# Sums of squares of the head norms in a two-block transformer kernel: one float32 matmul replaced by two fp32r matmuls of a split square

## The reference, cut to what matters

```
def _rms(x, g):
    xf = x.astype(jnp.float32)
    y = xf * lax.rsqrt(jnp.mean(xf * xf, axis=-1, keepdims=True) + EPS)
    return (y * g.astype(jnp.float32)).astype(x.dtype)

k = _rms(k, k_norm_g)                                      # 16 heads of 128, FoX keys
q = _rms(q.reshape(bsz, s, B_HEADS, HEAD_DIM), q_norm_g)   # 16 heads of 128, FoX queries
q = rms_norm(q.reshape(b, t, A_HEADS_2, HEAD_DIM_2), q_g)  # 8 heads of 64, second block
k = rms_norm(k.reshape(b, t, A_KV_HEADS, HEAD_DIM_2), k_g) # 2 heads of 64, second block
```

## Time and profile before

| | value |
|---|---|
| median of three runs | 1354.71 us (1353.22 to 1357.62) |
| profiled execution | 1361.22 us, its span 1359.5 us |
| TensorE matmul busy | 1253.9 us, 92% |
| DVE busy | 794.2 us, 58% |
| ACT busy | 613.7 us, 45% |
| POOL busy | 107.8 us, 8% |
| granted TensorE clock, mean | 0.958 of full |
| DMA | 219.93 MB, mean 162 GB/s |

### The profile page before, as it was taken

The page is one execution under the profiler, slowest core; times in us unless marked ns, Lnnn a source line. Parts: engine busy times, 40 slices in busy tenths (PEclk is TensorE's granted clock), DMA queues, the critical chain, the costliest instruction groups (busy, mean ns, idle before and its releaser), DMA issues.

```text
span 1359.5 us, 20850 instructions
## 1 busy us (share of the span) xinstructions
PE 1253.9 (92%) x8513; PEld 1146.1 (84%) x8513; DVE 794.2 (58%) x1257; ACT 613.7 (45%) x950; POOL 107.8 (8%) x172
## 2 busy tenths in 40 slices
PE   1799999898979899999989598999999999899998
PEld 1799999876878899887788378999989987899997
DVE  6786998654486354455446746555555433665554
ACT  2447623433455454554434335444444554544442
POOL 0100000022030000011100410000000133000000
PEclk9999999997979999999979688999999999899999
DMA  9796789501647556322532044555554321455552
GB/s 321 223 310 200 230 261 312 200 1 34 198 150 226 153 162 204 104 92 94 163 94 70 32 155 131 181 187 187 187 183 149 131 94 62 155 186 186 187 186 93
DMA packets 164879, 219.93 MB, mean 162 GB/s; under 512 B 5868, under 2 KB 135696, under 8 KB 164784
## 3 DMA queue, kind: packets, MB, share of 16 engines
q1 hardware_dynamic: 163984, 216.82, 49.3%
q0 software_dynamic: 800, 1.77, 0.4%
HBM read 217.53 MB, written 1.05 MB: 161 GB/s over the span
## 4 chain that ended last, share of the span: by engine, by line
PE 75%; DVE 11%; DMA 6%; ACT 5%; issue 2%; SPq 0%; DVEq 0%; ACTq 0%
PE ps L636 12%; PE ps L640 11%; PE ps L637 11%; PE ps L693 6%; PE ps L694 6%; PE ps L698 6%; DMA raw_weights<-in_a_w_in 3%; PE ps L666 3%; PE ps L667 3%; DVE w_lo L1543 3%; PE ps L671 3%; DVE acc L1626 2%; ACT w_hi L1223 1%; PE ps L924 1%; DMA raw_weights<-in_kv_w 1%
## 5 line engine op out<-in xcount | busy, mean ns | idle before, releaser
L1543 DVE TENSOR_TENSOR w_lo<-raw_weights,w_hi 128x1024 fp32r<-128x1024 f32 x348 | 423.9, 1229 | 291.4 <-ACT w_hi L1223 289.9
L1223 ACT ACTIVATE w_hi<-raw_weights 128x1024 fp32r<-128x1024 f32 x348 | 362.6, 1054 | 415.3 <-PE ps L698 110.3
L636 PE MATMUL ps<-act_hi,w_hi 128*128 128x256 f32 x1664 | 418.5, 289 | 6.4 <-ACT w_hi L1223 6.4
L637 PE MATMUL ps<-act_lo,w_hi 128*128 128x256 f32 x1664 | 410.1, 284 | 0.0
L636 PEld LDWEIGHTS ps<-act_hi,w_hi 128*128 128x128 f32 x1664 | 320.5, 193 | 14.1 <-issue 10.4
L637 PEld LDWEIGHTS ps<-act_lo,w_hi 128*128 128x128 f32 x1664 | 320.7, 193 | 3.5 <-issue 2.9
L640 PE MATMUL ps<-act_hi,w_lo 128*128 128x256 f32 x1664 | 234.7, 284 | 5.8 <-DVE w_lo L1543 5.8
L640 PEld LDWEIGHTS ps<-act_hi,w_lo 128*128 128x128 f32 x1664 | 215.5, 193 | 6.4 <-DVE w_lo L1543 6.4
L693 PE MATMUL ps<-w_hi,act_hi 128*128 128x512 f32 x360 | 142.7, 396 | 2.3 <-DVE work L1728 1.7
L694 PE MATMUL ps<-w_hi,act_lo 128*128 128x512 f32 x360 | 141.2, 392 | 0.0
L698 PE MATMUL ps<-w_lo,act_hi 128*128 128x512 f32 x360 | 99.2, 389 | 0.0
(11 more groups left out here) (252 smaller groups left out, 1295.6 us busy)
## 6 DMA issues: line engine op xcount, KB each, us to landing
raw_weights<-in_ffn_w SPq DMA_DIRECT2D x66, 1024.0 KB, 5.3
raw_weights<-in_a_w_in SPq DMA_DIRECT2D x32, 1024.0 KB, 6.1
raw_weights<-in_mod_w SPq DMA_DIRECT2D x24, 1024.0 KB, 5.8
raw_weights<-in_kv_w SPq DMA_DIRECT2D x16, 1024.0 KB, 5.8
raw_weights<-in_b_w_in SPq DMA_DIRECT2D x16, 1024.0 KB, 5.4
raw_weights<-in_od_w_qkv SPq DMA_DIRECT2D x12, 1024.0 KB, 5.1
raw_weights<-in_kv_mod_w SPq DMA_DIRECT2D x8, 1024.0 KB, 5.5
raw_weights<-in_a_w_out SPq DMA_DIRECT2D x8, 1024.0 KB, 4.9
```

The source lines that it names most:

```text
L636: pe.matmul(dst, wh[:, k, :], act_hi[:, base + k, :], start=(k == 0), stop=False)
L637: pe.matmul(dst, wh[:, k, :], act_lo[:, base + k, :], start=False, stop=False)
L1223: act.activation(half_view(w_hi, s), HALVES[s][2], ACT.Copy).then_inc(hi_done, 1)
L1543: dve.tensor_tensor(half_view(w_lo, s), HALVES[s][2], half_view(w_hi, s).bitcast(F32), ALU.subtract).then_inc(lo_done, 1)
```

## The change

TensorE gets two fp32r matmuls for each sum: the square rounded to fp32r, and the exact rest of it. POOL makes both, with a cast and a subtraction of 128x512. The rounded part has one buffer, the rest two, in the memory of `h_sq` and of the second `h_r` buffer, so `h_r` has one buffer left and ACT waits for the previous unit's read of it. The constant matrices become a tile of fp32r type, which is read as float32 where float32 is wanted; their first part is loaded on POOL's queue at the start of its program in place of SP's, the second part by two transfers in place of one.

```diff
+        cst_r = sb("cst_matrices", [P, 5 * P], F32R)
+        cst = sb("cst_rows", [P, const.shape[1] - 5 * P])
+        with nc.sbuf_tensor("work_rounded", [P, 3584], F32R) as work_r:
+            pass
...
-        h_r = work[:, 1024:2048].rearrange("p (b n) -> p b n", b=2)
+        h_r = work[:, 1024:1536]
+        h_sq_hi = work_r[:, 1536:2048]
+        h_sq_lo = work_r[:, 0:1024].rearrange("p (b n) -> p b n", b=2)
...
         @block.gpsimd
+            pool.dma_start(cst_r[:, 0:256], const[:, 0:256].bitcast(F32R)).then_inc(ident_in, 16)
...
-            pool.dma_start(cst[:, 256:], const[:, 256:]).then_inc(masks_in, 16)
+            pool.dma_start(cst_r[:, 256:], const[:, 256:640].bitcast(F32R)).then_inc(masks_in, 16)
+            pool.dma_start(cst[:, :], const[:, 640:]).then_inc(masks_in, 16)
...
-            for h in range(HA):
-                if h == KD:
-                    pool.wait_ge(unit_ready, FIRST["q"] + 8)
-                split_output(h, o_full[:, h % 2, :], st("fx_out"), st("fx_split"), fox_chunk(h))
+            def split_squares(n):
+                pool.wait_ge(st("hsq_ready"), n + 1)
+                if n >= 1:
+                    pool.wait_ge(st("hssq_ready"), n)
+                pool.tensor_copy(h_sq_hi, h_sq[:, n % 2, :]).then_inc(st("hsq_hi"), 1)
+                pool.wait_ge(st("hsq_hi"), n + 1)
+                pool.tensor_tensor(h_sq_lo[:, n % 2, :], h_sq[:, n % 2, :], h_sq_hi.bitcast(F32), ALU.subtract)\
+                    .then_inc(st("hsq_lo"), 1)
+            for n in range(8):
+                split_squares(n)
+            for i in range(2, HA + 6):
+                if i % 2 == 0 and i <= HA:
+                    split_squares(8 + (i - 2) // 2)
+                if i >= 6:
+                    h = i - 6
+                    if h == KD:
+                        pool.wait_ge(unit_ready, FIRST["q"] + 8)
+                    split_output(h, o_full[:, h % 2, :], st("fx_out"), st("fx_split"), fox_chunk(h))
+            for n in range(16, 19):
+                split_squares(n)
...
             def head_square_sums(mat, count):
-                pe.wait_ge(st("hsq_ready"), count + 1)
+                pe.wait_ge(st("hsq_lo"), count + 1)
...
-                pe.matmul(square_bank(count), mat, h_sq[:, count % 2, :], start=True, stop=True)\
+                pe.matmul(square_bank(count), mat, h_sq_hi, start=True, stop=False)
+                pe.matmul(square_bank(count), mat, h_sq_lo[:, count % 2, :], start=False, stop=True)\
                     .then_inc(st("hssq_ready"), 1)
...
         @block.sync
-            sp.dma_start(cst[:, 0:256], const[:, 0:256]).then_inc(ident_in, 16)
...
             def scale_unit(n, size):
-                if n >= 2:
-                    wait_read(act, *normed_units[n - 2])
+                if n >= 1:
+                    wait_read(act, *normed_units[n - 1])
...
-            dve.wait_ge(masks_in, 32)
+            dve.wait_ge(masks_in, 48)
```

More of the change, by code:

```diff
@@ L154, in build @@
         acc = sb("acc", [P, 2, HALF])
-        cst = sb("cst", [P, const.shape[1]])
+        cst_r = sb("cst_matrices", [P, 5 * P], F32R)
+        cst = sb("cst_rows", [P, const.shape[1] - 5 * P])
         att_mask = sb("att_mask", [P, 2, P], I32)
@@ L158, in build @@
         small = sb("small", [P, 256])
+        with nc.sbuf_tensor("work_rounded", [P, 3584], F32R) as work_r:
+            pass
         work = sb("work", [P, 3584])
[L161 to L165, removed]
+        ident_r, ones_r, ones64_r, neg_after_r, neg_ones_r = (cst_r[:, n * P:(n + 1) * P] for n in range(5))
+        ident, ones = ident_r.bitcast(F32), ones_r.bitcast(F32)
+        ones64, neg_after, neg_ones = ones64_r.bitcast(F32), neg_after_r.bitcast(F32), neg_ones_r.bitcast(F32)
+        causal = cst[:, 0:384]
+        chunk_go = cst[:, 384:640]
+        inv_count = cst[:, 640:704].rearrange("p (g t) -> p g t", g=4)
         def grid(n, heads=HA):
@@ L347, in build @@
                      "osq_ready ossq_ready orstd_ready o_used ot_ready "
-                     "hsq_ready hssq_ready hrstd_ready "
+                     "hsq_ready hsq_hi hsq_lo hssq_ready hrstd_ready "
                      "f_min f_ln nf_ready "
@@ L876, in _ @@
                 if n >= 1:
-                    head_square_sums(ones, n - 1)
+                    head_square_sums(ones_r, n - 1)
                 for m in mod_end.get(("kv", n), ()):
@@ L882, in _ @@
                 if n == 0:
-                    head_square_sums(ones, 7)
+                    head_square_sums(ones_r, 7)
             bank = open_unit("forget")
@@ L953, in _ @@
                 if i >= 3 and i % 2 == 1 and i <= 17:
-                    head_square_sums(ones, 8 + (i - 3) // 2)
+                    head_square_sums(ones_r, 8 + (i - 3) // 2)
                 if 5 <= i:
@@ L1035, in _ @@
             pe.wait_ge(st("ev_relu"), HIDX)
-            head_square_sums(ones64, 16)
+            head_square_sums(ones64_r, 16)
             project_features("ev_q", "ev_q", SELF)
             project_features("ev_q", "ev_q", SELF)
-            head_square_sums(ones64, 17)
+            head_square_sums(ones64_r, 17)
             project_features("ev_u", "ev_u", SELF)
-            head_square_sums(ones64, 18)
+            head_square_sums(ones64_r, 18)
             project_features("ev_u", "ev_u", SELF)
@@ L1372, in scale_unit @@
                 act.wait_ge(st("hssq_ready"), n + 1)
-                if n >= 2:
-                    wait_read(act, *normed_units[n - 2])
-                link(act.activation(h_r[:, n % 2, :], square_bank(n), ACT.Ln, scale=1.0 / size, bias=eps_t))
-                act.activation(h_r[:, n % 2, :], h_r[:, n % 2, :], ACT.Exp, scale=-0.5).then_inc(st("hrstd_ready"), 1)
+                if n >= 1:
+                    wait_read(act, *normed_units[n - 1])
+                link(act.activation(h_r, square_bank(n), ACT.Ln, scale=1.0 / size, bias=eps_t))
+                act.activation(h_r, h_r, ACT.Exp, scale=-0.5).then_inc(st("hrstd_ready"), 1)
             for i in range(8):
@@ L1773, in normed @@
                 dve.scalar_tensor_tensor(out=dst, in0=bank.rearrange("p (h t) -> p h t", h=2), scalar=gain,
-                                         in1=h_r[:, n % 2, :].rearrange("p (h t) -> p h t", h=2),
+                                         in1=h_r.rearrange("p (h t) -> p h t", h=2),
                                          op0=ALU.mult, op1=ALU.mult).then_inc(unit_free["v"], 1)
@@ L1855, in _ @@
                         out=qN[:, 2 * n:2 * n + 2, :], in0=bank.rearrange("p (h t) -> p h t", h=2), scalar=q_gain,
-                        in1=h_r[:, n % 2, :].rearrange("p (h t) -> p h t", h=2), op0=ALU.mult, op1=ALU.mult)\
+                        in1=h_r.rearrange("p (h t) -> p h t", h=2), op0=ALU.mult, op1=ALU.mult)\
                         .then_inc(unit_free["v"], 1)
```

## The result

The changed kernel takes 1361.93 us (median of 4 runs, 1360.23 to 1363.46), the kernel before 1354.03 (4 runs, 1353.22 to 1357.62) beside it. The ratio is 1.0053, with an interval of 1.0029 to 1.0077: slower by 3.9 to 10.4 us, most likely by 7. The forecast was 1355.8 with a range of 1350 to 1361.5; the median lies 0.4 us above the range, and 1354.03 x 1.0053 = 1361.2 just inside it. In some executions the granted clock is lower and the time more than 1.5% longer: all medians and ratios here leave them out, and of e1's trace, which is of such an execution, only the stretches behind 392 us are used.

What follows compares the result with a forecast made beforehand. It took TensorE (92% busy) and DVE's releases with DMA behind them as two loops at nearly one pace. Start -0.2, k +2.4, q -2.4, second block +1.3 gave +1.1: 1354.7 + 1.1 = 1355.8 us, range 1350 to 1361.5.

Steps and rivals of the forecast that it cites:

- The gain on TensorE: All 19 square sums: two fp32r matmuls in place of one float32, 0.40 us each, 7.6 us if nothing waits.
- D: Rival at the square sums: the fp32r pair takes as long as the float32 matmul, +6 us, 1361; chance 0.03.
- Start: Kernel start: identity on POOL's queue lets modulation pieces issue 0.4 us earlier, -0.2 us; +1 if it lands after 6.
- k stretch: k projections: splits delay DVE's modulation sums and make TensorE wait, +2.4 us, bounds +0.8 and +6.
- Sum 1: Second k square sum: waits for POOL's split and starts at 409.2 instead of 405.44, +3.8 us.
- wait at sum 3: Fourth k square sum: starts 4.0 us late for its split; would absorb clock lost behind the first gap.
- q stretch: q projections inside the attention: eight shorter sums less a last stall of 0.8 us, -2.4 us, bounds -3.2 and -1.
- Second block: Three sums beside DVE's top-64 choosing: splits delay DVE, TensorE's w_lo wait grows, +1.3 us, bounds -0.4 and +2.5.
- Rival B: k stretch: splits 0 to 4 each cost DVE 1.5 us through the slot loop; total +4.6, 1359.3; chance 0.24.
- A: Rival, whole kernel: POOL and DVE hinder each other little, only two late squares cost; -3.2, 1351.5; chance 0.22.
- C: Rival, whole kernel: all splits are hidden, -7.6 - 0.4, 1346.7; chance 0.05.

Runs made afterwards that it cites:

- e1: Changed kernel with POOL splitting only the eight q squares, the other sums one float32 matmul on the unsplit square: 1353.25 us, ratio 0.999.
- e7: Changed kernel without the exact rest: ACT writes rounded squares, POOL splits nothing, one fp32r matmul for each sum: 1345.82 us, ratio 0.994.
- e3: Kernel before with only the identity and the ones loaded on POOL's queue in place of SP's: 1354.95 us, ratio 0.9994.
- e4: Changed kernel with all 19 splits made but unused; TensorE does the float32 sum without waiting for POOL: 1361.03 us, ratio 1.0042.
- e5: Changed kernel with only the three squares of the second block split, k and q sums float32: 1359.67 us, ratio 1.0044.
- e11: e5 with 24 fp32r matmuls that nobody reads in front of TensorE's wait for w_lo: 1357.24 us, ratio 1.0007.
- e2: Changed kernel with the k and q squares split, the three sums of the second block float32: 1358.10 us, ratio 1.0004.
- e10: Changed kernel with only the two query squares of the second block (17 and 18) split: 1356.03 us, ratio 0.9984.
- e9: Changed kernel with only the first sum of the second block (16) split: 1355.22 us, ratio 0.999.

## Why the prediction was right and wrong

- **The gain on TensorE** (0.40 us a sum): 0.38, right. That the fp32r pair is no cheaper (D) is out: 395 and 397 ns records 0.23 apart, and e7's 0.60 for one matmul less.
- **Start** (-0.2, or +1 if the identity lands after 6): it landed at 6.99, and yet the matmul of 13.84 came at 13.34, and 0.35 earlier in e3. The term fits, the condition that I tied it to was not right: what ends last there is the transfer of a parameter row, which SP now issues earlier. In all eleven traces of kernels that load the identity on POOL's queue that matmul is 0.05 to 0.50 us earlier.
- **k stretch** (+2.4, bounds +0.8 and +6): +2.9, and 0.45 more behind it. Sum 1 is where it was put (409.0 against 409.2; wait 3.96). Behind sum 3 TensorE is 3.55 us later than at 400, the forecast was 3.6; but there is no wait at sum 3. I had written that clock lost behind the first gap would be eaten by the wait at sum 3; it is the other way round, the lost clock (0.66 over 5 us) was longer than the wait would have been. That the total is near the forecast is luck to that extent. e4 parts the term: DVE's delay 1.2, the wait for the split and the clock behind it the rest.
- **q stretch** (-2.4, bounds -3.2 and -1): -1.8. The stall at the last sum is +0.83 for a forecast of 0.8, by the very instruction named. The difference is 0.02 a sum, 0.12 at the first, whose split isn't quite ready (the forecast allowed 0 to 0.5), and the last sum's own gain of 0.4, which the same wait swallows; I had counted both.
- **Second block** (+1.3, bounds -0.4 and +2.5): +3.3, outside its bounds. This is the step that failed. Its first part held: split 16 on the w_lo (+0.70 for +0.75) and split 17 on the mask steps (+1.3 for +1.0), 2.0 us of DVE where I had 1.75. What failed is what follows from it. I had a gap of 3.42 us in the earlier trace rows with 1.6 us of clock lost behind it, used that price in the k stretch, and didn't apply it here, where my own sum made a gap of 1.68 + 1.75 = 3.4. It became 3.84, the clock fell to 0.53, and behind the gap 2.0 us more were lost (1.5 in e5), which e11, where the gap is filled, doesn't lose. And the 0.4 that the shorter sums were to give back isn't there at the end: sum 16's lengthens the gap, and of the 0.8 that sums 17 and 18 do give, half is gone again in the wait at the end of the block. e7 with 0.6 a sum gained nothing in this block.
- **Rival B** named a total near the result (1359.3), but not by what happened. It wanted every split from 0 to 4 to delay DVE by 1.5 us; over the kernel DVE lost 0.5 us a split, about 1 us was felt at the transfer behind split 0, and the k stretch stayed under the 5 us that would have shown B. A and C are out by e4 and by the wait at sum 1.
- **Chances and range.** I had given 0.60 to a difference too small to tell and 0.24 to slower; it came out slower, clear of noise. The forecast's own spread, 1353 to 1359, doesn't hold the result. The wider range reaches 1361.5 only because it left room for B, and B's mechanism wasn't the one.

The Trainium skill, "SBUF — State Buffer", section "Who interferes with whom", has DVE instructions with two SBUF inputs caught beside POOL. For SCALAR_TENSOR_TENSOR, which no row of before showed, the trace agrees: 1672 ns for 752.

**What stays open.** The stretches add up to +4.5 us, the medians differ by 7.9 (ratio: 7, 3.9 to 10.4). The sum lies inside the interval, but e5 too is 1.6 us (median) to 3 us (ratio) above what the block in its trace shows, and after against e2 gives the second block some 5 us by the medians and 6.6 by the ratios, where traces give 3.3. The intervals are wide enough for all of this. Each trace is one execution, and where the half-clock phases fall differs from one to the next: up to 7.6 us before 392 us, where all kernels do nearly the same work. It may be that a longer gap brings more such phases in other executions than in the profiled ones; no run here shows it. That e5 and e11 differ in the clock lost because of the gap is shown by one trace each; why e10's gap of 2.04 us was followed by a window at 0.75 and e9's of 2.55 by one at 1.00 is not.

## What to carry to other kernels

Work moved from the busiest engine to an idle one is paid where the idle one makes a third stand still, as POOL does with DVE here: price it as time of DVE at each place where it lands, and follow each delay to a wait of TensorE, then add the clock that the wait may cost. Move it only at the places where its input is early and DVE isn't feeding transfers: here 11 of 19 splits gain 5 us, all 19 lose 7. And don't subtract spans of single profiles when the clock phases of one execution differ by more than the effect; subtract stretches between the same instructions, over several kernels that share the stretch.

## What the runs showed of the hardware

- A tiny DVE instruction is caught for the whole of POOL's: 128x2 took 1.30 us beside a subtraction of 1.30 (0.17 alone). It has one SBUF input, so two inputs aren't needed for it; TENSOR_SCALAR of 128x512 took 1.53 us beside POOL's work, before and after, 0.47 alone.
- It goes both ways: the cast of 0.61 us took 1.25, the subtraction of 1.28 took up to 2.21.
- Behind gaps of TensorE of 3.96, 3.84 and 3.84 us (after twice, e5) the granted clock over the next 5 us was 0.66, 0.50 and 0.66. With matmuls that nobody reads in the gap (e11) it was 1.00, and the block was 1.2 us shorter than in e5. The length of the gap alone doesn't tell: 2.55 us cost no clock in e9, 2.04 us cost 1.4 us in e10.
